# Unread matmuls in four gaps of TensorE's work: a two-layer trunk with norms, a state-space layer and routed experts

## The reference

```python
h = rmsnorm(x, g) * (1 + scale) + shift      # _ada_norm, scale and shift from c
x = x + gate * mixer_or_ffn(h)
...
logits = h @ router_w + router_b             # second layer
top_p, top_i = top_k(softmax(logits), 2)
out = sum over e of gates[:, e] * swiglu_e(h)
```

## Time and profile before

| | us |
|---|---|
| median of 3 runs | 1543.82 (1540.29 to 1545.14) |
| profiled execution | 1538.52 |
| its span | 1536.7 |
| mean granted clock | 0.977 |
| TensorE matmul busy | 1436.9 (94%) |
| TensorE weight loads busy | 1086.1 (71%) |
| VectorE busy | 372.8 (24%) |
| ScalarE busy | 159.8 (10%) |
| GpSimd busy | 138.6 (9%) |

### The profile page before, as it was taken

The page is one execution under the profiler, slowest core; times in us unless marked ns, Lnnn a source line. Parts: engine busy times, 40 slices in busy tenths (PEclk is TensorE's granted clock), DMA queues, the critical chain, the costliest instruction groups (busy, mean ns, idle before and its releaser), DMA issues.

```text
span 1536.7 us, 44743 instructions
## 1 busy us (share of the span) xinstructions
PE 1436.9 (94%) x19890; PEld 1086.1 (71%) x19890; DVE 372.8 (24%) x1026; ACT 159.8 (10%) x382; POOL 138.6 (9%) x230
## 2 busy tenths in 40 slices
PE   5998999999997897799999989989989999999996
PEld 4886888888886786666667767767757767765553
DVE  2815240220203703211111111111111111122334
ACT  3103111111012203100000000000000000000001
POOL 0000042140300000000000000000000000000000
PEclk9999999999999998999999999999999999999998
DMA  9948496657519417349999999999999999998960
GB/s 388 422 159 318 164 367 234 248 203 290 192 65 395 171 42 309 142 165 369 426 426 411 426 426 411 427 426 409 427 425 417 416 426 423 416 425 368 373 279 28
DMA packets 44203, 493.91 MB, mean 321 GB/s; under 512 B 4897, under 2 KB 5153, under 8 KB 5793
## 3 DMA queue, kind: packets, MB, share of 16 engines
q1 hardware_dynamic: 41040, 475.02, 75.5%
q10 hardware_dynamic: 3024, 16.73, 2.7%
HBM read 478.10 MB, written 13.63 MB: 320 GB/s over the span
## 4 chain that ended last, share of the span: by engine, by line
PE 81%; DMA 12%; DVE 4%; issue 1%; ACT 1%; SPq 0%; POOLq 0%; POOL 0%; DVEq 0%
PE PS L720 29%; PE PS L429 20%; PE PS L729 14%; DMA ring<-in_expert_stream 7%; PE PS L583 5%; DMA arena<-in_expert_stream 4%; PE PS L418 2%; DMA ring<-in_dense_stream 2%; PE PS L738 1%; PE PS L700 1%; PE PS L632 1%; DVE arena L1025 1%; PE PS L553 1%; PE PS L565 1%; PE PS L461 1%
## 5 line engine op out<-in xcount | busy, mean ns | idle before, releaser
L720 PE MATMUL PS<-ring,arena 128*32 128x256 f32 x7040 | 406.0, 381 | 26.0 <-DMA ring<-in_expert_stream 14.2
L720 PEld LDWEIGHTS PS<-ring,arena 128*32 128x32 f32 x7040 | 257.7, 110 | 153.1 <-issue 21.7
L429 PE MATMUL PS<-arena,ring 128*128 128x256 f32 x1408 | 310.1, 380 | 5.0 <-ACT arena L828 2.7
L729 PE MATMUL PS<-ring,arena 128*32 128x256 f32 x4928 | 298.5, 380 | 0.8 <-DVE consts L1025 0.8
L429 PEld LDWEIGHTS PS<-arena,ring 128*128 128x128 f32 x1408 | 265.8, 190 | 44.5 <-issue 7.1
L729 PEld LDWEIGHTS PS<-ring,arena 128*32 128x32 f32 x4928 | 184.2, 111 | 84.9 <-issue 3.6
L720 PE MATMUL PS<-arena 128*32 128x256 f32 x2816 | 163.6, 383 | 6.7 <-DMA arena<-in_expert_stream 5.5
L1025 DVE TENSOR_TENSOR stat<-stat,PS 128x128 f32<-128x128 f32 x154 | 44.3, 288 | 508.1 <-ACT stat L982 508.1
L1025 DVE TENSOR_TENSOR arena<-arena,PS 128x256 f32 (+1 forms) x123 | 55.3, 449 | 376.0 <-PE PS L429 236.4
L720 PEld LDWEIGHTS PS<-arena 128*32 128x32 f32 x2816 | 106.7, 111 | 54.7 <-DMA arena<-in_expert_stream 6.4
L1563 POOL COPY arena<-arena 128x256 f32 x153 | 61.3, 401 | 813.5 <-PE PS L720 764.9
(11 more groups left out here) (180 smaller groups left out, 620.4 us busy)
## 6 DMA issues: line engine op xcount, KB each, us to landing
ring<-in_expert_stream SPq DMA_DIRECT2D x136, 2048.0 KB, 19.2
ring<-in_dense_stream SPq DMA_DIRECT2D x105, 1024.0 KB, 7.2
arena<-in_expert_stream SPq DMA_DIRECT2D x32, 2048.0 KB, 22.8
ssm_scratch<-arena ACTq DMA_DIRECT2D x12, 1024.0 KB, 4.9
ring<-ssm_scratch SPq DMA_DIRECT2D x12, 1024.0 KB, 17.0
arena<-in_xt ACTq DMA_DIRECT2D x1, 1024.0 KB, 14.0
arena<-in_ssm_small ACTq DMA_DIRECT2D x1, 1024.0 KB, 10.3
out_t<-arena ACTq DMA_DIRECT2D x4, 256.0 KB, 2.6
```

Source lines behind the costliest of these rows:

```text
L429: mm = pe.matmul(PS[:, bank, j * T:(j + 1) * T], w[:, c, j * P:(j + 1) * P], moving[:, c, :], start=(c == 0), stop=(c == NC - 1))
L720: mm = pe.matmul(PS[32 * q:32 * q + 32, 0, 0:256], hbuf[:, c * BLK:(c + 1) * BLK], w[:, q * 256:(q + 1) * 256], start=(c == 0), stop=(c == ...
L729: mm = pe.matmul(PS[32 * q:32 * q + 32, 1, 0:256], hidT[:, ch * BLK:(ch + 1) * BLK], w[:, q * 256:(q + 1) * 256], start=(ch == 0), stop=(c ...
```

## The change

A helper `spin(n, bank)` issues n matmuls with the identity as stationary and the first 256 columns of the constants as moving operand. Each starts a new sum in a PSUM bank, and nothing reads that bank before it is written again. It is called in four places of TensorE's program: 16 matmuls after the sums of the state-space layer's norm, 9 after the sums of the routing's norm, 9 between the position matmuls and the gather, and 9 between the last scatter and the sums of the final norm. There is no new semaphore and no other edit.

```diff
@@ -418,6 +418,11 @@
+            def spin(n, bank):
+
+                for _ in range(n):
+                    pe.matmul(PS[:, bank, 0:T], ident, consts[:, 0:T], start=True, stop=True)
@@ -607,6 +612,7 @@
             sums(2, 0)
+            spin(16, 1)
             pe.wait_ge(h_ready, 3 * NC)
@@ -666,6 +672,7 @@
             sums(3, 0)
+            spin(9, 3)
             for c in range(NC):
                 pe.wait_ge(h_ready, 3 * NC + c + 1)
@@ -791,6 +799,7 @@
             scatter(last=True)
 
+            spin(9, 2)
             sums(4, 0)
```

## The result

| | before | after |
|---|---|---|
| median, us | 1542.68 (8 runs, 1538.04 to 1548.29) | 1534.22 (8 runs, 1532.57 to 1540.77) |
| profiled execution, us | 1538.52 | 1535.29 |
| its span, us | 1536.7 | 1533.5 |
| mean granted clock | 0.977 | 0.985 |

The account below looks back on a forecast made before the run. TensorE was taken to bound the kernel outside the weight-streamed expert stage, with gains ahead of and after the stream counting in full. Terms 1.9 + 1.9 + 0.2 + 1.6 = 5.6 us led from 1543.82 to 1538.2 us, range 1534.3 to 1543.5.

Parts of the forecast that it names:

- rival (c): Expert stage: its start is not what TensorE frees, so only the fourth gap counts, 1.6 us, 1542.2 us; chance 0.08.
- First gap: State-space norm's sums to L618 and L632: 16 matmuls keep the clock high, +1.9 us, bounds -0.4 to 4.1.
- The -0.4: First gap: the 16 matmuls end at 497.0 us, 0.4 us after L618 now starts.
- The term for L618: First gap: L618's 128 instructions go from 34 to 27 ns apart at 2.4 GHz, +0.9 us.
- Second gap: Routing norm's sums to the router chunks (L672): nine matmuls hold the clock for most chunks, +1.9 us, bounds -0.4 to +2.5.
- 1.3 chunks stay low: Second gap: clock falls at about 605 us, so 1.3 router chunks stay low instead of six, 0.47 us each.
- Third gap: Position matmuls to gather: nine matmuls start low, delay the gather but spare it 2.3 us; +0.2 us, bounds -1.9 to +0.6.
- Fourth gap: Last scatter to final norm's sums: nine matmuls hidden by VectorE's residual make the sums high, +1.6 us, bounds -0.5 to +2.3.
- the sum against one execution: Whole kernel: 5.6 us off the profiled 1538.52 gives 1532.9; adding its 5.3 us below the median gives 1538.2.
- (a): Routing: the clock holds through it as well, 9.2 us in all, 1534.6 us; chance 0.12.
- (b): All gaps: the clock falls again soon after each filling, some 2.6 us in all, 1541.2 us; chance 0.27.
- (d): All gaps: filling matmuls neither hold nor raise the clock, -9.7 us, 1553.5 us, slower; chance 0.04.

Follow-up runs that it names:

- only_routing: The kernel before with only the two fillings of 9 in the routing, after the routing norm's sums and ahead of the gather: 1538.94 us, 0.9962 of before.
- no_third: The changed kernel without the 9 matmuls between the position matmuls and the gather: 1534.25 us, 0.9934 of before.
- shaped: Changed kernel with fillings of 15, 9, 8 and 9, plus 5 during VectorE's pick and 4 between the last scatters: 1531.46 us, again 1532.76 us; 0.9927, 0.9915 of before.

## Why the prediction was right or wrong

**What bounds the kernel: right.** The gains ahead of the stream reached the end; rival (c), that the stream hides them, would have left only_routing at the time of before, and it was 0.38% faster. DMA was empty ahead of the stream in the changed kernel as well (0.00 from 622 to 636 us), and the stream moved as forecast: SP issues its next load 147.9 us after the first sums of 489.24, at 637.18, where it was 152.5 us in the kernel before (638.14 against 485.67):

```profile
637.18 2.06 SPq L366 DMA_DIRECT2D ring<-in_expert_stream  x2
```

These 4.5 us are what the two norm stretches and the gaps up to the first expert matmul gave in this pair (1.57 and 2.97).

**First gap, +1.9: near.** 1.3 on average. The -0.4 was 0.5 to 0.6. The term for L618 was mis-sized: I took 27 ns between matmuls, 0.9 us, and it was (2.76 - 0.37) / 128 = 18.6 ns, 1.8 us. The Trainium skill, page "TensorE: Matmul & The Clock Gate", section "Wait — 56ns, not 53.3ns?", gives a floor of about 25 ns between starts, and this row is below it; the measurement decides. Nor was L643 evidence of a floor: its matmuls start four at a time, 6 to 7 ns apart, and then 89 ns pass, so that its 27 ns is a mean over such groups, and L618 itself had starts 7 ns apart in the kernel before. The bigger mistake stood beside it: the 1.4 us for L632's first 2.8 us at the low level. That was the particular execution: L632 takes 15.82 us in it, and 14.48 in the five others without this filling.

**Second gap, +1.9: mis-sized.** The step "1.3 chunks stay low" and the pitch of 0.70 us failed. I had read 0.70 off the one pair of chunks at the high level; with the clock held they are 0.62 us apart. And I counted the clock's fall from the end of the filling, with the delays of idle stretches. The router's matmuls and transposes did not raise it, but it outlasted them: in the five executions with this filling and none in the pick the clock fell 5.7 to 8.0 us after the filling gave way to the first router matmul, always behind the last chunk (in the changed kernel at 610.2 us, 7.9 after 602.3); in one execution of shaped it fell among the chunks, after 3.6 us. From the first router matmul to the first position matmul it is 7.58 us with filling and 11.1 on average without: 3.5 less, 0.3 of it lost in front: 3.2 instead of 1.9, and above the upper bound of 2.5.

**Third gap, +0.2: right.** -0.2 in the trace, and no difference in time between the kernels with and without it. The mechanism is the one forecast: started low, it is late by about what it gives back. (The table's second row gives 0.4 us more than the second gap's 3.2; that holds in no_third as well, so it is not this filling's.)

**Fourth gap, +1.6: right**, 2.0 on average, between 0.1 and 3.0 by where the clock was lost.

**Left out: the hole of register reading behind the gather.** I had its 3.4 us in front of me as the gap between the gather and L720, and took it as unchanged. In the first execution of before the clock stayed up through it; in five others it did not, at 2.8 us each. With the fillings 1.8 us less are lost there on average (1.4 over all seven executions with a filled routing).

**The step that failed is the sum against one execution**: "It lies 5.3 us below the median, and the median of the changed kernel should be 1538.2". I carried the 5.3 us over as if they had nothing to do with the change. Part of them were low stretches that this execution happened not to have, in the first expert block (2.8) and in the tail (1.4), and the fillings take much of those away too; against them it had 1.1 us more than the others in the first stretch. With the stretches averaged over six executions the sum is 8.8 (the rounded terms give 8.7) instead of 5.6. In the forecast's own terms:

| term | forecast, us | on average, us |
|---|---|---|
| first gap | +1.9 | +1.3 |
| second gap | +1.9 | +3.2 |
| third gap, to the first expert matmul | +0.2 | +0.4 |
| register reading and first expert block | not in the sum | +1.8 |
| fourth gap | +1.6 | +2.0 |

So the two terms that failed are the second gap, mis-sized by 1.3 us, and the hole of register reading, put at nothing. The forecast median was 4.0 us too high: 2.9 us of that is the gain (5.6 for a measured 8.5), and 1.1 us is the median of before, which came down from 1543.82 over three runs to 1542.68 over eight. By the measured ratio, 1543.82 would have led to 1535.0, so the last tenth outside the range is chance. The forecast's 5.6 us lie just inside the interval of the measured gain (5.2 to 12.5); that the gain is larger rests on the stretches above and on the later runs of the changed kernel (0.9939). The range was also said to begin at (a), whose own time is 1534.6, not 1534.3.

**The rivals.** (a), the clock holds all through: partly so; it held through the chunks but not through the pick, and with shaped's five extra matmuls it did in one execution of two. Its time, 1534.6, was the nearest of all, partly by luck: it had 2.0 us in the third gap, which gave nothing, and nothing for the register reading. (b), it falls soon: refuted by every execution with filling, none of which lost the clock in L618 or after one or two chunks. (d): refuted by the result.

## What to carry to other kernels

Where TensorE waits some microseconds between stretches that matter, unread matmuls of 256 columns cut to the length of the hole kept its clock, and ones of 8 columns did not; they must start while it is still high, since one that starts low is late for the real work by what it spares. Look for every hole that is behind the last filling, register reads included. Before summing what a change does to the clock, profile several executions of the kernel before: where the clock falls moved one stretch by up to 2.9 us from execution to execution, as much as a filling is worth.

## What the runs showed of the hardware

- 128 f32 matmul instructions on 32x32 tiles, 256 columns, come 18.6 ns apart on average at 2.4 GHz and 30.5 ns at 1.2 GHz ((4.53 - 0.63) / 128). Single starts on different tiles are 6 to 7 ns apart.
- Router matmuls with 8 columns and transposes, busy 7.3 us on end, did not raise the clock from 0.50, but where they followed a filling they ran for the 5.1 us of all eight chunks at 1.00 in seven of eight executions. Work that does not raise a low clock can run to its end at a high one.
- Eight register reads left TensorE idle for 3.4 us between the gather and L720; moved ahead of the gather they took up to 5.7 us (609.83 to 615.52), and the idle time there grew from 3.6 to 6.65 us.
- Two executions of the changed kernel's expert stage, 7 rounds against a stream at 422 GB/s, differed by 7 us (877.7 and 884.6).
